# The adaLN modulation of a two-layer block: ada_w multiplied raw, in four column groups, folded in batches

## The reference

```python
silu_c, silu_cc = silu(c), silu(c_ctx)
for i in range(2):
    mod_l = silu_c @ ada_w[i] + ada_b[i]      # ada_w[i]: 1024 x 6144
    mod_c = silu_cc @ ada_w[i] + ada_b[i]
    sh1, sc1, g1, sh2, sc2, g2 = split(mod, 6)
    a = rms_norm(h, norm_mix[i]) * (1 + sc1) + sh1
    h = h + g1 * mixer(a)                     # layer 0: neighbourhood attention, 1: grouped-query attention
    h = h + g2 * swiglu_ffn(rms_norm(h, norm_ffn[i]) * (1 + sc2) + sh2)
```

## Time and profile before

| | us |
|---|---|
| timed runs, median (lowest, highest) of 3 | 1749.7 (1748.64, 1750.54) |
| the profiled execution, its own time | 1752.67 |
| its span | 1751.1 |
| PE busy | 1670.9 |
| DVE busy | 1007.0 |
| ACT busy | 755.1 |

### The profile page before, as it was taken

One profiled execution on the slowest core, in us unless ns is written; L12 is line 12 of the kernel. 1 busy time (PEld: TensorE's weight loads), 2 busy tenths in 40 slices (PEclk: granted clock), 3 DMA queues, 4 the chain that ended last, 5 costly groups with the idle time before them and its releaser, 6 DMA issues.

```text
span 1751.1 us, 26382 instructions
## 1 busy us (share of the span) xinstructions
PE 1670.9 (95%) x11395; PEld 1471.3 (84%) x11395; DVE 1007.0 (58%) x1310; ACT 755.1 (43%) x957; POOL 82.1 (5%) x124
## 2 busy tenths in 40 slices
PE   6999989979999999998989899998799999999998
PEld 3688966767887888886967899998799999999998
DVE  3544467556554554435666655556577755567763
ACT  2432367435332333223556444453455444454543
POOL 4000034000000000000000000004100000000000
PEclk9999999989999999998999899999899999899999
DMA  9645433233454454322210455564355555355552
GB/s 250 220 162 175 145 49 31 73 121 121 144 186 151 144 168 169 115 78 96 97 49 27 137 176 192 175 204 152 126 176 186 185 177 187 103 183 178 191 170 73
DMA packets 242980, 251.31 MB, mean 144 GB/s; under 512 B 4797, under 2 KB 240672, under 8 KB 242864
## 3 DMA queue, kind: packets, MB, share of 16 engines
q1 hardware_dynamic: 240112, 244.34, 41.9%
q0 software_dynamic: 2464, 5.09, 2.6%
q10 hardware_dynamic: 288, 0.19, 0.0%
HBM read 248.55 MB, written 1.05 MB: 143 GB/s over the span
## 4 chain that ended last, share of the span: by engine, by line
PE 91%; DVE 5%; DMA 2%; ACT 1%; issue 1%; SPq 0%; DVEq 0%; ACTq 0%
PE psum L317 89%; PE psum L753 2%; DMA raw<-in_ada_w 2%; DVE wl L300 1%; DVE sums L816 1%; DVE pt L830 1%; ACT wh L293 1%; DMA raw<-in_na_w_qkv 0%; DVE acc L974 0%; DVE acc L1414 0%; DVE hT L982 0%; ACT scr L783 0%; DVE proj L1698 0%; DVE xl L473 0%; DVE scr L463 0%
## 5 line engine op out<-in xcount | busy, mean ns | idle before, releaser
L300 DVE TENSOR_TENSOR wl<-raw,wh 128x2048 fp32r<-128x2048 f32 (+1 forms) x226 | 509.0, 2253 | 243.0 <-ACT wh L293 242.4
L317 PE MATMUL psum<-xh,wh 128*128 128x256 f32 (+1 forms) x1936 | 617.5, 319 | 11.9 <-DVE xl L473 7.0
L317 PE MATMUL psum<-xl,wh 128*128 128x256 f32 (+1 forms) x1936 | 613.5, 317 | 0.0
L317 PE MATMUL psum<-xh,wl 128*128 128x256 f32 (+1 forms) x1936 | 613.1, 317 | 0.0
L293 ACT ACTIVATE wh<-raw 128x2048 fp32r<-128x2048 f32 (+1 forms) x226 | 423.2, 1881 | 405.4 <-PE psum L317 402.6
L317 PEld LDWEIGHTS psum<-xh,wh 128*128 128x128 f32 x1936 | 375.2, 194 | 40.4 <-issue 12.2
L317 PEld LDWEIGHTS psum<-xh,wl 128*128 128x128 f32 x1936 | 374.9, 194 | 22.7
L317 PEld LDWEIGHTS psum<-xl,wh 128*128 128x128 f32 x1936 | 375.2, 194 | 21.8 <-issue 0.5
L317 PE MATMUL psum<-ah,wh 128*128 128x256 f32 (+1 forms) x704 | 218.0, 310 | 0.0
L317 PE MATMUL psum<-al,wh 128*128 128x256 f32 (+1 forms) x704 | 217.9, 310 | 0.0
L317 PE MATMUL psum<-ah,wl 128*128 128x256 f32 (+1 forms) x704 | 217.9, 309 | 0.0
(11 more groups left out here) (242 smaller groups left out, 1773.7 us busy)
## 6 DMA issues: line engine op xcount, KB each, us to landing
raw<-in_ada_w SPq DMA_DIRECT2D x48, 1024.0 KB, 5.2
raw<-in_ffn_w_in SPq DMA_DIRECT2D x44, 1024.0 KB, 4.9
raw<-in_w_ffn_gate SPq DMA_DIRECT2D x22, 1024.0 KB, 5.0
raw<-in_w_ffn_up SPq DMA_DIRECT2D x22, 1024.0 KB, 5.0
raw<-in_ffn_w_out SPq DMA_DIRECT2D x16, 1024.0 KB, 5.1
raw<-in_w_ffn_down SPq DMA_DIRECT2D x16, 1024.0 KB, 5.1
raw<-in_na_w_qkv SPq DMA_DIRECT2D x12, 1024.0 KB, 4.9
raw<-in_w_in_even SPq DMA_DIRECT2D x8, 1024.0 KB, 5.2
```

Source lines behind the costliest of these rows:

```text
L300: dve.e.tensor_tensor(wl[:, n % NSPL, 0:z], raw[:, c % NRAW, 0:z], wh[:, n % NSPL, 0:z].bitcast(F32), ALU.subtract).then_inc(W.lo, 1)
L317: return pe.e.matmul(o, l, r, start=start, stop=stop, skip_group_check=shared)
```

## The change

No ada chunk is split any more. All 48 are multiplied in fp32 from `raw`. The eight row tiles of a chunk go, in two rounds, to the four column groups of the array, each 32 columns wide: row tile 4r+j writes partitions 32j to 32j+31 of the PSUM bank. The weights are a window of 32 columns of `cz`, a tile (in rstd) that is zero but for the two condition columns; shifting the window by 2q puts the result of a batch's q-th chunk in rows 2q and 2q+1, and the other rows get zeros added. So up to 12 chunks gather in one bank. One copy of 128 x 256, one fold with the matrix `four` (it picks a row and sums the four groups) and one add serve a whole batch: eight batches of one in setup, then chunks 8 to 19 (LATE), 20 to 23 (GATES), 24 to 35 (NEXT), 36 to 47 (LAST). LATE is copied ahead of attention and folded behind it. The chunks stand behind weight groups as before, one each behind all twelve groups of qkv0, two of o0 and 20 of the first feed-forward; three stand in each of the two norm gaps, two ahead of the column sums and one behind the spread. A slot of `raw` with an ada chunk is free once PE has used it. The load order puts an ada chunk behind the weight chunk two places further on. The coefficients of the next norm are made earlier, in o0 and in the feed-forward.

```diff
-        adas = rstd[0:4, :].rearrange("p (a n) -> p a n", a=2)
+        cz = rstd[:, :].rearrange("p (k n) -> p k n", k=KT)
+        four = sb("four", [P, 32])
+        adas = sb("adas", [P, 256])[:, :]
...
+        ADA = [(0, i) for i in (0, 4, 1, 5, 2, 6, 3, 7)] + [(0, i) for i in range(8, 24)] + [(1, i) for i in range(24)]
+        BATCHES = [[a] for a in range(8)] + [range(8, 20), range(20, 24), range(24, 36), range(36, 48)]
+        LATE, GATES, NEXT, LAST = 8, 9, 10, 11
+        after = {i: [8 + i] for i in range(14)}
+        after[first_ffn0 - 1] = [22, 23, 24]
+        after.update({first_ffn0 + i: [25 + i] for i in range(20)})
+        after[first_qkv1 - 1] = [45, 46, 47]
+        dma = [("ada", a) for a in range(8)]
+        for c in range(NW):
+            dma.append(("w", c))
+            dma += [("ada", a) for a in after.get(c - AHEAD, ())]
...
+                    if kind_before == "ada":
+                        sp.wait_ge(A.used, before + 1)
+                    else:
+                        sp.wait_ge(W.hi, before + 1)
+                        sp.wait_ge(W.lo, before + 1)
...
         def ada_mm(a):
-            if a < RAW:
-                x = sc.rearrange("p (s k) -> p k s", s=2)
-                for k in range(KT):
-                    last = mm(ada_bank(a)[0:2, 0:256], x[:, k, :], w[:, k, :], k == 0, k == KT - 1)
-            else:
-                h, l = taken(c)
-                for k in range(KT):
-                    mm(ada_bank(a)[0:4, 0:256], cm[:, k, :], h[:, k, :], k == 0, False)
-                    last = mm(ada_bank(a)[0:4, 0:256], cm[:, k, :], l[:, k, :], False, k == KT - 1)
+            for r in range(2):
+                for j in range(4):
+                    k = 4 * r + j
+                    last = mm(ada_bank(b)[32 * j:32 * j + 32, 0:256], cz[:, k, 30 - 2 * q:62 - 2 * q], w[:, k, :], r == 0 and q == 0,
+                              r == 1 and q == len(BATCHES[b]) - 1)
...
+        def ada_fold(b):
+            n = 2 * len(BATCHES[b])
+            pe.wait_ge(A.copied, b + 1)
+            for m in range(2):
+                last = mm(ada_bank(b)[:, 256 + n * m:256 + n * m + n], adas[:, m * P:(m + 1) * P], four[:, 0:n], True, True)
...
         def attention0_pe():
+            pe.wait_ge(A.copied, LATE + 1)
...
         def o0_pe():
+            ada_fold(LATE)
...
+            gap = after[where["o0", 3]]
+            ada_mm(gap[0])
+            ada_mm(gap[1])
             pe.wait_ge(O0.sum, KT - 1)
             stat_pe(1, 4)
+            spread_pe(1, 4)
+            ada_mm(gap[2])
```

More of the change, by code:

```diff
@@ L197, in cols, with stage @@
             return (w[k0 * P:(k0 + nk) * P, c0:c0 + n].rearrange("(k p) n -> p k n", p=P), nk, n)
[L199 to L222, removed]
+        weights, where = [], {}
+        def stage(name, chunks):
+            steps = [(name, i) for i in range(len(chunks))]
+            for step, src in zip(steps, chunks):
+                where[step] = len(weights)
+                weights.append(src)
             return steps
@@ L239, in program @@
[L239 to L251, removed]
@@ L252, in program @@
-        NCHUNK = len(order)
-        aidx = {m: a for a, m in enumerate(ADA)}
+            st_ffn0.append((stage(f"up0{n}", up_chunks(ins["ffn_w_in"][0], ins["ffn_w_in"][0], 0, FF, range(a, b))),
+                            stage(f"dn0{n}", down_chunks(ins["ffn_w_out"][0], [(2 * a, 2 * (b - a))]))))
+        stage("qkv1", [cols(ins["gqa_w_qkv"][0], 256 * i) for i in (4, 0, 1, 2, 3, 5)])
+        stage("o1", [cols(ins["gqa_w_o"][0], 256 * i) for i in range(4)])
+        stage("up1", up_chunks(ins["ffn_w_in"][1], ins["ffn_w_in"][1], 0, FF, range(11)))
@@ new lines, in program @@
+        aidx = {m: place[a][0] for a, m in enumerate(ADA)}
+        first_ffn0, first_qkv1 = where["up00", 0], where["qkv1", 0]
+        after = {i: [8 + i] for i in range(14)}
[6 more added lines that the diff above has]
+            dma += [("ada", a) for a in after.get(c - AHEAD, ())]
@@ L257, in program, with view, ada_src @@
+        assert [a for kind, a in dma if kind == "ada"] == list(range(48))
+        pos = {x: p for p, x in enumerate(dma)}
         s_raw = [nc.alloc_semaphore(f"w_raw{i}") for i in range(NRAW)]
         W = semaphores(nc, "w", "hi lo used")
[L260 to L265, removed]
+        def view(t, slot, src):
+            _, nk, n = src
             return t[:, slot, 0:nk * n].rearrange("p (k n) -> p k n", n=n)
+        def ada_src(a):
+            l, i = ADA[a]
+            return cols(ins["ada_w"][l], 256 * i)
@@ L272, in sync_program @@
                 sp.e.dma_start(dst, src).then_inc(L.x, 16)
[L273 to L280, removed]
+            for p, (kind, x) in enumerate(dma):
+                if p >= NRAW:
+                    kind_before, before = dma[p - NRAW]
+                    if kind_before == "ada":
[3 more added lines that the diff above has]
+                        sp.wait_ge(W.lo, before + 1)
+                src = ada_src(x) if kind == "ada" else weights[x]
+                sp.e.dma_start(view(raw, p % NRAW, src), src[0]).then_inc(s_raw[p % NRAW], 16)
             sp.wait_ge(FIN.yd, 2)
@@ L326, in group_T @@
             shared = n == T
-            total = sum(order[c][1] for c in cs)
+            total = sum(weights[c][1] for c in cs)
             ks = ks or list(range(total))
@@ L539, in setup_pe @@
                 last.then_inc(X.turned, 1)
-            for a in range(RAW):
+            for a in range(8):
                 if a:
@@ L1078, in ffn0_act @@
                     split_for(split_hi, where[step])
-                    if third == 2 and step[0] != "ada" and step[1] >= 1:
+                    if third == 2 and step[1] >= 1:
                         squares_act(G0, step[1] - 1, 2, 32)
```

285 lines of the change are left out of this document (138 added, 147 removed).

## The result

The changed kernel took 1688.9 us (median; 1688.8 to 1690.9) beside 1750.1 for the kernel before on the same chip: ratio 0.965, 95% interval 0.964 to 0.967, clearly faster. The forecast was 1681.0 with a range of 1671 to 1713, so the time lies inside the range and 7.9 us above the forecast. Run again on another occasion, the ratio was 0.965 again (0.964 to 0.967). The profiled execution's span is 1687.6, against 1751.1 before: 63.5 less, where 68.7 were forecast.

What follows compares the result with a forecast made beforehand. TensorE, 95% busy, was taken to bound the kernel. Gains of 57.1 + 4.1 + 4.2 + 3.3 = 68.7 us took the profiled 1752.7 to 1684.0, or 1681.0 against the timed median 1749.7; range 1671 to 1713.

Steps and rivals of the forecast that it cites:

- Four abreast, 1.05 per chunk: Ada chunks: four column groups run at once, 0.87 plus two shape changes of 0.09, 1.05 us against 2.47; chance 0.62.
- rival 1: Ada chunks: only two calls run abreast, 1.92 us per chunk, 1711 us in all; chance 0.15.
- Rival 2: Ada chunks: four abreast with a loss of a fifth or so, 1.28 us per chunk, 1689 in all; chance 0.12.
- rival 3: Ada chunks: nothing abreast in groups of 32, 3.65 us per chunk, 1780 in all, slower; chance 0.08.
- Dense chunks, 57.1: qkv0, o0 and feed-forward: 38 chunks at 2.47 become 33 at 1.05 plus four folds, gaining 57.1 us.
- qkv0 to attention, 4.1: Last qkv0 group to attention: 5.8 us becomes 1.7 without the VectorE split ahead of the copy, gaining 4.1.
- the first gap, 4.2: o0 to feed-forward: 17.0 us becomes 12.8 as in the second gap, chunks fitting in idle time, gaining 4.2.
- Setup, 3.3: First eight chunks: faster slot rounds bring 4.7 us, less 1.4 for low clock in the first group; bounds 0 to 8.
- Clock in the gaps and attention, counted as nothing: Norm gaps: with chunks inside, the clock may fall later; nothing counted, bound 3 us gained per gap.
- rival 4: Weight groups: loads fall behind as group plus chunk takes 11.9 instead of 13.4 us; perhaps 20 us, 1700; chance 0.03.
- qkv1's wait: qkv1's third group waits for an add that VectorE does one group earlier: 0 to 2 us.
- The step from the sum to the timed median: Profiled run, 3.0 above the timed median: 1752.7 less 68.7 is 1684.0, so 1681.0 against the median 1749.7.

Runs made afterwards that it cites:

- one- and two-group kernels: Changed kernel with all eight row tiles in column group 0, or alternately in groups 0 and 1, instead of four groups: 1779.4 us and 1714.8 us.
- full-width kernel: Changed kernel with eight calls of full-width weights (128 columns), nothing abreast, array never narrowed: 1766.2 us, ratio 1.008 to the kernel before.
- split_back: Changed kernel with a VectorE subtraction the size of a removed split put back before the qkv0-end copy and in the first norm gap: 1697.6 us.
- warm: Changed kernel with idle-time matmuls of a constant by the identity behind setup chunks 3 to 7 only: 1688.8 us, ratio 0.964 to the kernel before.
- pairs: Changed kernel with the dense-stretch chunks two by two behind every second weight group, 30 chunks at 15 places: 1686.0 us, ratio 0.963.
- warm_all: Changed kernel with idle time filled by matmuls to the setup's end and in both gaps, first weight's split behind the last setup copy: 1684.4 us.

## Why the prediction was right, and where it was off

- **Four abreast, 1.05 per chunk.** Right: 1.09. The step from two groups in a row of before to four held exactly. Rivals 1, 2 and 3 needed 1.92, 1.28 and 3.65. The one- and two-group kernels show that rivals 3 and 1 had their price right (1779 and 1715, against 1780 and 1711) and their condition wrong. Rival 2 is a warning: its 1689 is the measured time, and its 1.28 is nearly the full price of 1.26. Its reason is not what happened, since no slot is longer than 0.216. The time alone could not have told it from the forecast's mechanism; the timeline does.
- **Dense chunks, 57.1.** The term that was mis-sized: it left out the slow restart. 33 chunks cost 0.04 + 0.165 = 0.2 more than reckoned, 6.8 us in all, which is most of what qkv0 and the feed-forward lack in the table. The full-width kernel shows that 0.31 of each chunk's 1.26 comes from going to 32-column tiles and back. The prediction took 0.18 for it, from a row (pt, vtok) after which a 64-row matmul follows, so that the way back to full width was never in view. The 0.09 ahead of the fold in the earlier trace rows, which I read as the same price, fitted in number.
- **qkv0 to attention, 4.1, and the first gap, 4.2.** Right to a tenth, and split_back shows that VectorE's splits held them up. The other part of each (ScalarE's split before attention, the copy and its wait in the gap) was only argued.
- **Setup, 3.3.** Mis-sized, and by the wrong mechanism. 3.0 was won at the start of the first group, less 1.9 for that group's 12.78 us at clock 0.85 instead of 10.9, so about 1.1. The forecast took a third of a slot's round, load included, as the step of the setup. But before, the step from 49.83 to 54.49 was 3.62 of matmuls, 0.51 of wait for the copy and 0.53 of fold, together the 4.66, with no wait for a load. In the changed kernel three steps took 3.43, near the 3.6 reckoned, and that is luck: the chunk runs at half clock, 1.94 instead of 1.07, the fold too, and in two of the three PE waits between them for the copy (from 22.4 us to the end of the setup the mean clock was 0.95 before and is 0.50 now; the forecast saw the low clock coming, but priced it in the first group alone):

```profile
45.37 1.01 PE L318 MATMUL psum<-four,adas 128*128 128x2 f32 x4 [0.55 <-DVE adas L397]
```

At full clock, in warm, such a step took 2.40 (43.14 to 45.54). One step took 7.6, and that one did wait for a load. The chain that ended last shows what the setup hangs on, first in the changed kernel, then before (start, us, what):

```profile
25.88 13.54 DMA raw<-in_ada_w
44.89 5.67 DMA raw<-in_na_w_qkv
52.52 2.29 DVE wl L302
...
29.55 10.94 DMA raw<-in_ada_w
48.83 5.10 DMA raw<-in_na_w_qkv
```

The ada load was asked for 3.7 us earlier and landed only 1.1 earlier, at 39.42. The forecast had kept the median time to landing for a faster taker, and this is what that median did (DMA rows of the first 62 us: issues, KB, median us to landing, which answer to the earlier trace rows; it was 9.2 before):

```profile
raw<-in_ada_w SPq DMA_DIRECT2D x9, 1024.0 KB, 11.9
```

From 39.42 on five loads landed 2.7 to 2.9 us apart (the last at 50.56), with the DMA engines busy 0.94 of the time, so an earlier request found the others still under way; that this made it wait longer is likely and was not tested. Behind it came two chunks, the load of the first weight and its two splits, and VectorE's split stands ahead of the last copy, as it did before, so the last fold waited for it:

```profile
55.27 1.01 PE L318 MATMUL psum<-four,adas 128*128 128x2 f32 x4 [3.21 <-DVE adas L397]
```

- **Clock in the gaps and attention, counted as nothing.** It gave 2.1 in attention (99.56 instead of 101.70) and 1.5 in the first group behind the gap (12.29 instead of 13.76). That attention's clock held because PE is idle 2 us less ahead of it fits split_back, but pairs and warm_all show a fall with the short wait as well. The rest took 0.8 back beyond its fold. Across the kernels with the changed program's rest, the same instructions each time, it took between 921.1 (one group) and 926.5 us (pairs, split_back); what decides it was not found.
- **Loads (rival 4) and qkv1's wait.** No load made PE wait outside the setup, as reckoned.
- **The step from the sum to the timed median.** The forecast took 3.0 off because the profiled execution before lay that much above its median. The changed kernel's lay on its median (1688.8 and 1688.9). So what was missed beyond the 5.2 of the sum, some 2.7 of the 7.9 us, comes from there.

In sum, against 68.7: -6.8 (restart and the 0.04), -2.2 (setup), +2.1 and +1.5 (clock), -0.8 (rest), and +1.0 left over, about half of it the folds (a place with a fold takes 0.36 more than one without, not 0.53). That is 63.5. The clock's 3.6, which the forecast did not count, made up for part of what it had wrong; without them the miss would have been larger. Two of its figures do not add up: 0.9 on five chunks is 4.5 and not 4.7, and the low edge with the clock kept in both gaps and a setup of 8 is 1670 and not 1672.

## What to carry over

When a matmul needs few weight columns, give its row tiles to different column groups: with 8 tiles, one, two, three and four groups took 16, 8, 6 and 4 slots, and the order in which the calls are written did not matter. Price the tiling by what follows it as well: look at the spacing of the first matmuls behind the 32-column stretch, and put such work together at few places. Before a step is priced by a load's time, look whether the engine waits for a load in it at all. And in a kernel bound by TensorE look at the clock behind each wait as well as at the wait's own length. In the gaps here, work put into the wait, or even idle multiplying up to its very end, kept the clock.

## What the runs showed of the hardware

- Calls for four column groups start 7 ns apart and share a slot of 0.216 us; written group by group they start 13 ns apart and still share it.
- Going from full width to 32-column tiles costs 0.09 us and coming back 0.22, half of it ahead of the first full-width matmul and half in one slow spacing behind it (0.34 instead of 0.227). Full-width fp32 calls between the same matmuls cost none of it.
- In the setup a load asked for 3.7 us earlier landed 1.1 us earlier: its time to landing went from 10.9 to 13.5 us, with the DMA engines busy 0.94 of the time.
- The clock fell to half (1.2 GHz) after idle stretches and once, in warm, fell just after work had come back. Filling that stopped 2.8 us early won nothing. With filling up to the end and the reordered split, the first group ran at 1.00.
